# Output projection and the first key/value and query chunks as seven block products per pair of token tiles

## The reference

```
# end of first_block
y = jnp.concatenate([y_ssm, y_attn], axis=-1) @ w_out[l]
x = x + gate[:, None, :] * y
# beginning of second_block
h = rms_norm_2(x, attn_norm_w)
z = h @ w_in                      # pool inputs, q, kv, gates
q = rope(rms_norm_2(q, q_norm_w), pos) * SCALE
k = rope(rms_norm_2(kv[:, :, :, 0], k_norm_w[:, None, :]), pos)
```

## Time and profile before

| | us |
|---|---|
| median of 3 runs | 1329.15 |
| lowest and highest | 1328.39, 1332.79 |
| profiled execution, its own time | 1328.42 |
| its span in the profile | 1326.6 |
| TensorE busy in the span | 1295.8 |
| VectorE busy | 882.6 |
| ScalarE, GpSimd busy | 364.6, 270.2 |

### The profile page before, as it was taken

How to read it: one execution, slowest core, us unless ns; L and a number is a source line. 1 busy time by engine, 2 the same in 40 slices (tenths; PEclk the granted TensorE clock), 3 DMA queues, 4 the chain that set the end, 5 groups by cost and what they waited for, 6 DMA issues and landing times.

```text
span 1326.6 us, 16164 instructions
## 1 busy us (share of the span) xinstructions
PE 1295.8 (98%) x5696; PEld 882.3 (67%) x5696; DVE 882.6 (67%) x2050; ACT 364.6 (27%) x900; POOL 270.2 (20%) x264
## 2 busy tenths in 40 slices
PE   4999999999999999999999999999999999999998
PEld 3444555544544544886555556888888888888887
DVE  5898999679331465465456676676767767777564
ACT  4222121225200102222456676111223332330000
POOL 1168568215003287700000000000000000000000
PEclk9999999999999999999999999999999999999999
DMA  9773425651312112302103002212323223224210
GB/s 322 205 135 120 142 40 159 199 173 40 119 38 78 64 64 64 127 32 95 65 1 64 1 1 52 76 64 60 116 64 125 67 65 126 64 91 148 84 53 32
DMA packets 91036, 120.59 MB, mean 91 GB/s; under 512 B 16488, under 2 KB 52654, under 8 KB 90956
## 3 DMA queue, kind: packets, MB, share of 16 engines
q1 hardware_dynamic: 86256, 110.81, 27.4%
q10 hardware_dynamic: 2956, 5.05, 1.2%
q0 software_dynamic: 1744, 3.70, 0.9%
HBM read 111.00 MB, written 6.84 MB: 89 GB/s over the span
## 4 chain that ended last, share of the span: by engine, by line
PE 89%; DVE 5%; SPq 2%; DMA 2%; issue 1%; ACT 1%; POOL 0%; DVEq 0%; ACTq 0%; POOLq 0%
PE bank L1504 18%; PE bank L875 12%; PE bank L1530 10%; PE bank L888 9%; PE bank L1432 7%; PE bank L1390 6%; PE bank L910 5%; PE bank L1163 4%; PE bank L1273 4%; PE bank L1344 3%; PE bank L1370 3%; PE bank L1208 2%; SPq L705 2%; PE bank L1475 2%; DMA arena<-in_w_in 2%
## 5 line engine op out<-in xcount | busy, mean ns | idle before, releaser
L1504 PE MATMUL bank<-arena 128*128 128x256 f32 x1120 | 241.9, 379 | 0.0
L1504 PEld LDWEIGHTS bank<-arena 128*128 128x128 f32 x1120 | 213.3, 190 | 28.4
L875 PE MATMUL bank<-arena 128*128 128x512 f32 (+1 forms) x384 | 157.0, 566 | 0.0
L1530 PE MATMUL bank<-arena 128*128 128x256 f32 x616 | 133.1, 379 | 0.0
L888 PE MATMUL bank<-arena 128*128 128x512 f32 x288 | 127.7, 596 | 0.0
L1530 PEld LDWEIGHTS bank<-arena 128*128 128x128 f32 x616 | 117.3, 190 | 15.7
L910 PEld LDWEIGHTS bank<-arena 128*128 128x128 f32 (+2 forms) x660 | 77.8, 143 | 71.3 <-issue 45.1
L875 PEld LDWEIGHTS bank<-arena 128*128 128x128 f32 x384 | 72.1, 190 | 77.6 <-issue 73.5
L910 PE MATMUL bank<-arena 128*128 128x128 f32 (+2 forms) x660 | 93.2, 279 | 19.9 <-ACT arena L1614 7.2
L2918 DVE CUSTOM_DVE_ANT_0 arena<-bank,arena 128x128 f32<-128x128 f32 (+3 forms) x128 | 57.6, 487 | 67.6 <-PE bank L1344 66.2
L1432 PE MATMUL bank<-arena 128*128 128x256 f32 x448 | 97.6, 380 | 0.0
(11 more groups left out here) (388 smaller groups left out, 1953.9 us busy)
## 6 DMA issues: line engine op xcount, KB each, us to landing
arena<-in_w_in SPq DMA_DIRECT2D x14, 2048.0 KB, 7.9
arena<-in_w_up SPq DMA_DIRECT2D x20, 1024.0 KB, 6.9
arena<-in_w_ada SPq DMA_DIRECT2D x16, 512.0 KB, 9.1
arena<-in_w_down SPq DMA_DIRECT2D x8, 1024.0 KB, 7.5
arena<-in_w_out SPq DMA_DIRECT2D x2, 2048.0 KB, 9.8
arena<-in_w_attn_br SPq DMA_DIRECT2D x8, 512.0 KB, 8.4
arena<-in_w_o SPq DMA_DIRECT2D x2, 2048.0 KB, 8.5
rb_dram<-rb_one_dram ACTq DMA_DIRECT2D x1, 2560.0 KB
```

Source lines behind the costliest of these rows:

```text
L875: mm = pe.matmul(ps[:, 0:n], act[:, k, 128 * t:128 * t + 128], w[:, k, 0:n], start=(k == 0), stop=(k == kt - 1))
L1504: mm = pe.matmul(ps, left[:, k, :], right[:, k, :], start=(first and k == 0), stop=(k == 3), skip_group_check=True)
L1530: mm = pe.matmul(down_acc(i, name), left, right, start=first and name in ("P1", "P7", "P2", "P4"), stop=last, skip_group_check=True)
```

## The change

Each pair of token tiles (256 rows) and each chunk of 512 columns is one group of a 2 by 2 by 2 block scheme (Winograd's form of Strassen's): rows in two tiles, the 1024 inner values in two halves of 512, columns in two halves of 256. Seven products P1 to P7 take the place of eight. Each is four matmuls of 128 by 128 with 128 by 256, so a group has 28 of these, where it had 32 of 512 columns per pair. There are ten groups: 0 to 3 are the output projection, 4 and 5 kv1, 6 and 7 q2a, 8 and 9 q2b.

VectorE forms the sums of weights (block_sum, four instructions of 1024 elements for each of five chunks, one of them in place in the weights) and the sums of activations (row_sum, four of 512 elements for each of four tile pairs). ScalarE copies P1, P5, P7 and P6 from PSUM (row_copies). VectorE combines them (row_first and row_second) and for groups 0 to 3 applies gate and x in two instructions of 1024. P6 is summed onto P1 in its bank, P3 onto P5, P4 onto P7.

The copies of q2a and q2b to SBUF on ScalarE go away, since the combinations write there. The norm of keys is split in two (the first two of three, then the third), that of queries in four, one for each pair of tiles. GpSimd treats each pool input as it comes instead of after all four. A few semaphores that were used once are merged with others.

```diff
+            def row_products(g, *names):
+
...
+                    left, right, s_n, t_n = {
+                        "P1": (A[0][0], B[0][0], 0, 0), "P2": (A[0][1], B[1][0], 0, 0), "P5": (s1, t1, 1, 1),
+                        "P7": (s3, B[0][1], 2, 2), "P6": (s2, t2, 3, 3), "P3": (s4, B[1][1], 4, 0),
+                        "P4": (A[1][1], t4, 0, 4)}[name]
+                    if name == "P1" and g < 4:
+                        pe.wait_ge(ys_done, TT)
...
+                            for a in range(2):
+                                aux_out(pe, ("h2", t, a))
...
+                    if t_n:
+                        pe.wait_ge(rt_done, t0 + t_n)
+                    fresh = name in ("P1", "P2", "P5", "P7")
+                    if fresh:
+                        ps = begin_proj(("r", g, name))
+                    else:
...
+                        pe.wait_ge(rcopy_done, 4 * g + {"P6": 1, "P3": 2, "P4": 3}[name])
+                        ps = pbank(("r", g, name))
+                    for k in range(4):
+                        mm = pe.matmul(ps[:, 0:256], left[:, k, :], right[:, k, :], start=(fresh and k == 0), stop=(k == 3),
+                                       skip_group_check=True)
+                    mm.then_inc(proj_done, 1)
+
+            ALL = ("P1", "P2", "P5", "P7", "P6", "P3", "P4")
...
                 if n == NS1:
                     pe.wait_ge(lg_done, 2 * NS1)
...
-                    out_part(0, 0, (4, 5))
+                    row_products(0, "P1", "P2")
                 if n == NS1 + 1:
...
-                    out_part(0, 0, (6, 7))
+                    row_products(1, "P1")
...
+            row_products(0, "P5", "P7", "P6", "P3", "P4")
+            row_products(1, "P5", "P7", "P6", "P3", "P4")
+            row_products(2, *ALL)
+            for t in (0, 1):
+                row_turn("h2", xn2, t, (xn_done, TT + t + 1))
+            row_products(3, *ALL)
+            row_products(4, *ALL)
+            for t in (2, 3):
+                row_turn("h2", xn2, t, (xn_done, TT + t + 1))
+            one_rows("kv2", 0, "kv2", hT, 304)
+            one_rows("kv2", 1, "kv2", hT, 304)
+            row_products(5, *ALL)
+            one_rows("kv2", 2, "kv2", hT, 304)
+            one_rows("kv2", 3, "kv2", hT, 304)
+            for g in range(6, 10):
+                row_products(g, *ALL)
...
+            def row_copies(g):
+
+                if g >= 2:
+                    act.wait_ge(rgroup_done, g - 1)
+                for n, name in enumerate(("P1", "P5", "P7", "P6")):
+                    proj_ready(act, ("r", g, name))
+                    ins = act.activation(cR[g % 2][n], pbank(("r", g, name))[:, 0:256], ACT.Copy)
+                    ins.then_inc(rcopy_done, 1)
+                act.wait_ge(rcopy_done, 4 * g + 4)
...
+            for g in range(5):
+                row_copies(g)
...
+            def row_sum(m, part):
+
...
+                                aux_out(v, ("h2", t, a))
+                    ins = v.tensor_tensor(s1, A[1][0], A[1][1], ALU.add)
+                elif part == 1:
+                    ins = v.tensor_tensor(s3, A[0][0], A[1][0], ALU.subtract)
+                elif part == 2:
...
+            def block_sum(m, part):
+
...
+                t1, t2, t4 = tR[m]
+                if part == 0:
+                    ins = v.tensor_tensor(t1, B[0][1], B[0][0], ALU.subtract)
+                elif part == 1:
...
+                    ins = v.tensor_tensor(B[0][1], B[1][1], B[0][1], ALU.subtract)
+                elif part == 2:
...
+                    ins = v.tensor_tensor(t2, B[1][1], t1, ALU.subtract)
+                else:
...
+                    ins = v.tensor_tensor(t4, B[1][0], t2, ALU.subtract)
+                ins.then_inc(rt_done, 1)
...
+            def row_first(g):
+
...
+                    v.wait_ge(x1_done, g)
+                v.wait_ge(rcopy_done, 4 * g + 1)
+                proj_ready(v, ("r", g, "P2"))
+                for dst, cols in row_dest(g, 0, 0):
+                    v.tensor_tensor(dst, c[0][:, cols], pbank(("r", g, "P2"))[:, cols], ALU.add)\
+                        .then_inc(pfree(("r", g, "P2")), 1)
+                v.wait_ge(rcopy_done, 4 * g + 3)
+                step(v.tensor_tensor(c[2], c[2], c[1], ALU.add))
...
+            def row_second(g):
+
+                c = cR[g % 2]
...
+                v.wait_ge(rcopy_done, 4 * g + 4)
+                for dst, cols in row_dest(g, 1, 1):
+                    v.tensor_tensor(dst, c[3][:, cols], c[2][:, cols], ALU.add)
+                proj_ready(v, ("r", g, "P3"))
+                for dst, cols in row_dest(g, 0, 1):
+                    ins = v.tensor_tensor(dst, c[3][:, cols], pbank(("r", g, "P3"))[:, cols], ALU.add)
+                ins.then_inc(pfree(("r", g, "P3")), 1)
+                proj_ready(v, ("r", g, "P4"))
+                for dst, cols in row_dest(g, 1, 0):
+                    step(v.tensor_tensor(dst, c[3][:, cols], pbank(("r", g, "P4"))[:, cols], ALU.add))
+                v.sem_inc(pfree(("r", g, "P4")), 1)
+                v.sem_inc(rgroup_done, 1)
+                if g < 4:
+                    cols = slice(512 * j, 512 * j + 512)
+                    step(v.tensor_tensor(yR, yR, gate_b[:, cols].unsqueeze(1).broadcast_to((128, 2, 512)), ALU.mult))
...
+                    v.wait_ge(x_again[q], 16)
+                    xs = xrow[:, 2 * q:2 * q + 2, cols]
...
+
             v.wait_ge(bias_in, 16)
             for n in range(NS1 + 4):
...
                         fill1(kind, j)
+                else:
+                    block_sum(0, n - NS1)
+                    row_sum(0, n - NS1)
...
 
+            for part in range(4):
+                block_sum(1, part)
+            row_first(0)
+            row_second(0)
+            row_first(1)
+            for part in range(4):
+                row_sum(1, part)
+            block_sum(2, 0)
+            block_sum(2, 1)
+            row_second(1)
+            v.wait_ge(x1_done, 2)
+            row_square(0, xn2[:, 0, :])
+            row_square(1, xn2[:, 1, :])
+            row_first(2)
+            row_scaled_one(xn2, 0)
...
+            block_sum(2, 2)
+            block_sum(2, 3)
+            row_second(2)
...
+            for part in range(4):
+                row_sum(2, part)
+            row_first(3)
+            row_second(3)
+            v.wait_ge(x1_done, 4)
+            row_square(2, xn2[:, 2, :])
+            row_square(3, xn2[:, 3, :])
+            row_first(4)
+            row_scaled_one(xn2, 2)
+            row_scaled_one(xn2, 3)
+            row_second(4)
...
+            for part in range(4):
+                row_sum(3, part)
+            for part in range(4):
+                block_sum(3, part)
+            row_first(5)
+            row_second(5)
...
+            v.wait_ge(rgroup_done, 6)
+            key_norm(0, 2)
+            row_first(6)
...
+            key_norm(2, 3)
...
+            for part in range(4):
+                block_sum(4, part)
+            row_second(6)
+            row_first(7)
+            head_norm("q2a", gq2, qgain_done, row2, (0, 1), sq=sq2)
+            row_second(7)
+            row_first(8)
+            head_norm("q2a", gq2, qgain_done, row2, (2, 3), sq=sq2)
+            row_second(8)
+            row_first(9)
+            head_norm("q2b", gq2, qgain_done, q2b, (0, 1), sq=sq2)
...
-            head_norm("q2a", gq2, qgain_done, row2, sq=sq2)
-            head_norm("q2b", gq2, qgain_done, q2b, sq=sq2)
+            row_second(9)
+            head_norm("q2b", gq2, qgain_done, q2b, (2, 3), sq=sq2)
```

More of the change, by code:

```diff
@@ L574, in program @@
         pool_ones = sem("pool_ones")
-        u_saved = sem("u_saved")
         U_in = sem("U_in")
@@ L1853, in _ @@
                    .then_inc(pfree(("kv2", t)), 1)
-            rows_in_("q2a", row2)
-            rows_in_("q2b", q2b)
+            for g in range(5):
+                row_copies(g)
+            act.wait_ge(x1_done, 4)
+            act.dma_start(posr[0:32, :], cmp_pos_2[0].rearrange("a (k p) d -> (a k) (p d)", p=2)).then_inc(small_in, 16)
+            for c0 in (0, 64):
+                act.dma_start(w2s[:, c0:c0 + 64], cmp_w2_2[0, 0]).then_inc(small_in, 16)
+            act.dma_start(w2s[:, 128:192], cmp_w2_2[0, 1]).then_inc(small_in, 16)
+            kv2_in(0)
+            kv2_in(1)
+            row_copies(5)
+            kv2_in(2)
+            kv2_in(3)
+            for g in range(6, 10):
+                row_copies(g)
             def up_in(j):
@@ L2214, in rope @@
                 return pool.tensor_tensor(hi, t4[2], t4[3], ALU.add)
-            proj_ready(pool, ("kv1", 3))
+            proj_ready(pool, ("r", 5, "P4"))
             pool.memset(kcT[:, :, 2, :], 0.0).then_inc(kc_zero, 1)
@@ new lines, in block_sum @@
+            def block_sum(m, part):
+                key = (("out", 0), ("out", 1), "kv1", "q2a", "q2b")[m]
+                if key == "kv1":
+                    v.wait_ge(kv1_in, 16)
+                    w = w3
+                else:
```

(24 more changed lines are left out.)

223 lines of the change are left out of this document (125 added, 98 removed).

## The result

| | before | after |
|---|---|---|
| median of the runs | 1330.59 us (8 runs) | 1335.69 us (8 runs) |
| lowest and highest | 1328.39, 1332.79 | 1333.81, 1338.01 |
| profiled execution, its own time | 1328.42 | 1335.93 |

The changed kernel is slower by 0.4%: its time is 1.004 of the time before, 95% interval 1.003 to 1.005, so the loss is small but clear of the noise. The forecast was 1326.8 us, within 1317 to 1333; the time lies outside the range and on the other side.

A forecast was written before the change was run, and what follows sets the result against it. TensorE was taken to bound the kernel. 17.0 us shed less 12.8 of stalls and 1.9 of slow clock gave 2.3 us gained: 1326.1 us profiled, 1326.8 us as median, range 1317 to 1333.

The forecast's parts named there:

- What TensorE sheds: TensorE's ten product groups: 137.3 us become 120.8, 16.5 less; with the removed 0.48 us wait 17.0 in all.
- What VectorE gets: VectorE's added sums, combinations and roots: busy time up about 62 us to 945; ScalarE's copies add 8 us and hide.
- Early groups hidden: Groups 0 to 5: VectorE serves TensorE in time, smallest slack 1.4 us, cost nothing.
- Groups 6 to 9 not hidden: TensorE waits for VectorE's P3 bank at P5 of groups 7 to 9: 7.3, 2.3, 3.2, total 12.8 us.
- After group 9 the turned keys need kcd, ready at about 505 ... Both hidden: After group 9: key copies ready about 505, wanted 509.8; query rotation ends near 527, wanted 539; no wait.
- I take the 1.9 us once: TensorE's clock after the 7.3 us stall: slower work costs 1.9 us, counted once, bounds 0 and 5.
- the likeliest case: The forecast itself, whole kernel: a gain of 0 to 5 us, spanning 1324 to 1330 us, chance 0.50.
- The 0.84 us stays: TensorE's wait at the last turned queries, behind VectorE's sums over the m00 weights: 0.84 us, unchanged.
- slower than before: Rival, roots in groups 6 to 8: small VectorE instructions lose every turn to GpSimd, 14.9 us more, 1341.7 us; chance 0.18.
- The rival of the clock at every stall: Rival, groups 7 to 9: TensorE's slow clock is paid behind each stall, 3 us more, 1330 us; chance 0.10.

The follow-up runs named there:

- early groups alone: Changed kernel with both query chunks again as rows of eight products, without their weight sums, copies and combinations; 1318.28 us.
- rotation of one head: Changed kernel with GpSimd's rotations cut to one head of 64 columns, part of the result left out; 1320.53 us.
- Convolution copies early: Changed kernel with VectorE's two convolution-weight copies ahead of key copies and last query norms, TensorE's three small turns ahead of two up columns; 1330.04 us.
- new order, copies late: The new order without its last part: convolution copies stay behind all norms, small turns behind the two up-projection columns; 1328.64 us.
- gaps filled: Changed kernel with 33 matmuls that nobody reads put on TensorE where it stood idle; 1328.85 us.
- one set of sums early: Changed kernel with only group 6's last sums on VectorE moved ahead of the third key norm and block sums; 1337.14 us.
- new order: Changed kernel with key norms before group 6, each group's last sums before the previous group's query norm, convolution copies and small turns earlier; 1315.79 us.

## Why the prediction was wrong, point by point

- **What TensorE sheds: right.** With no stalls in its way the change is worth 16.3 us in the stretch (forecast 17.0).
- **What VectorE gets: right.** 939.7 us busy (forecast 945), ScalarE 372.7 (8 more, as forecast).
- **Early groups hidden: right.** No gap from 351.5 to 452.8, and "early groups alone" gives their share in full.
- **Groups 6 to 9 not hidden: right in place, near in size.** 6.55, 1.95, 2.36 us against 7.3, 2.3, 3.2; 10.9 against 12.8. The turns with GpSimd have 5.2 of it ("rotation of one head"), against the 6.3 counted.
- **"After group 9 the turned keys need kcd, ready at about 505 ... Both hidden": this step failed.** The copies of the keys were there (509.1), but a transpose also needs a bank. The walk of the queues followed the data of these transposes and not the banks that they write. It thereby missed the copies that empty two of these banks. They stand behind the last query norm, as before the change, but that norm now ends at 520.2 in place of 512.8 us, with VectorE busy almost without a break from 495.9 on: a wait of 4.65 us. "Convolution copies early" and "new order, copies late" show it from both sides, 5.65 us back and 12.9 lost.
- **"I take the 1.9 us once": mis-sized.** The clock was paid behind the first stall (14.04 for 12.25), the second (14.01) and the missed wait (24 transposes in 4.71 us, in 2.84 where the gap was filled). That is 5.4 us; by the pieces of "gaps filled" it is 5.3. The upper bound of the term was 5, and the likeliest case carried only the first stall. That 1.9 fits each of the three places is in part luck: it was read at one place of one profile, and there the same 32 transposes take from 5.04 to 6.61 us in the ten profiles.
- **"The 0.84 us stays": off by 0.8.** It is 1.64 us after. The m00 weights land as said (7.84 us for 7.75), but VectorE's four sums over them take 0.7 us more, since they meet GpSimd; the prediction counted no turns there.

The sum with the measured terms: -17.0 + 10.9 + 4.65 + 5.4 + 0.8 = 4.8 us, against 5.1 between the medians and 5.7 in the stretch. So of the 7.1 us from the forecast's -2.3 to this 4.8, 4.65 are the missed wait, 3.5 the clock (1.9 of them behind the missed wait), 0.8 the last queries, and -1.9 the stalls, which were shorter than forecast.

The rival "slower than before" named another mechanism, small instructions that lose every turn. In the changed kernel they don't: of the 55 instructions of the roots from 447 to 517 us all but one (0.55) took 0.17 or 0.18 us. The rival of the clock at every stall was the nearest to what happened. Its clock cost, 1.9 and 3 more, is near the measured 5.4, but 1.9 of this stand behind the wait that it didn't have, and the third stall cost nothing. Without the missed wait and its slow transposes the measured terms give a gain of 1.8 us, no change within what can be told.

## What to carry to other kernels

For each instruction whose engine is to be kept busy, follow all that it waits for, the bank or buffer that it writes as well as what it reads; when a queue gets more work or a new order, look at every later instruction on it which frees something, also at those whose place in the order is unchanged. An engine that waits on another's written order doesn't gain from one step brought forward: order the queue by when each result is wanted, and price a wait on TensorE with the slow products behind it. A cheap step left at the end of a tightened order costs more than in the slack one (11.18 us for 4.65).

## What the runs showed of the hardware

How long a wait must be before the clock falls isn't told by its length alone. A stall of 1.95 us was followed by slow products (14.01 for 12.32 us) and one of 2.36 us in the same kernel was not (8.87 us for 40 records); with one set of sums early, 2.37 us at the same place was (10.56 for 40). With the copies early, 1.96 us cost nothing and 2.87 us did (10.54 for 40).

In the new order some roots of the norms do meet GpSimd, and small instructions lose their turns. In its profile one of 128 x 16 takes 0.65 us beside a rotation instruction, where it takes 0.17 alone:

```profile
505.99 0.65 DVE L2346 SCALAR_TENSOR_TENSOR arena<-arena 128x16 f32<-128x16 f32 x1
506.68 0.65 DVE L2347 SCALAR_TENSOR_TENSOR arena<-arena 128x16 f32<-128x16 f32 x1
...
509.77 0.17 DVE L2347 SCALAR_TENSOR_TENSOR arena<-arena 128x16 f32<-128x16 f32 x1
```

```profile
505.88 0.73 POOL L2287 TENSOR_TENSOR arena<-arena 128x256 f32<-128x256 f32 x1
506.57 0.72 POOL L2288 TENSOR_TENSOR arena<-arena 128x256 f32<-128x256 f32 x1
```

The Trainium skill (SBUF — State Buffer, Who interferes with whom) says that a VectorE instruction with two SBUF inputs contends with a GpSimd instruction that reads SBUF, and these rows agree. The price here goes by GpSimd's instruction and not by VectorE's own: a small one that loses its turn ends with one of GpSimd's, 0.5 us on 0.17, and the root of eleven, four of which lost no turn, took 5.4 us in place of 2.3. "Rotation of one head" fits: sums of 1024 took 1.22 to 1.27 us beside GpSimd's instructions of 32 columns, and 1.55 to 1.74 in the changed kernel beside those of 256. GpSimd stays near its 0.72. In the changed kernel the roots happened to fall where GpSimd was silent, but for the one instruction of 0.55.
